# Attention's weights stay unscaled and are turned by a product with a diagonal matrix of reciprocal sums

## The reference

```python
# branch a (window_attention)
e = jnp.exp(s - m)
pr = e / (jnp.sum(e, axis=-1, keepdims=True) + jnp.exp(sk - m))
o = jnp.einsum('bnkgqs,bnskd->bnqkgd', pr.astype(v.dtype), v)
# branch b (dsa_attention)
pr = jax.nn.softmax(s, axis=-1)
o = jnp.einsum('bqkgs,bqskd->bqkgd', pr.astype(vg.dtype), vg)
```

## Time and profile before

| | |
|---|---|
| median of three runs | 1047.68 us |
| span of the profiled execution | 1044.9 us |
| PE busy | 930.3 us, 89% |
| PEld busy | 599.2 us, 57% |
| DVE busy | 394.1 us, 38% |
| ACT busy | 260.4 us, 25% |
| POOL busy | 123.1 us, 12% |
| attention | 162.4 to 257.2 us |

### The profile page before, as it was taken

The page is one execution under the profiler, slowest core; times in us unless marked ns, Lnnn a source line. Parts: engine busy times, 40 slices in busy tenths (PEclk is TensorE's granted clock), DMA queues, the critical chain, the costliest instruction groups (busy, mean ns, idle before and its releaser), DMA issues.

```text
span 1044.9 us, 14060 instructions
## 1 busy us (share of the span) xinstructions
PE 930.3 (89%) x5627; PEld 599.2 (57%) x5630; DVE 394.1 (38%) x1071; ACT 260.4 (25%) x529; POOL 123.1 (12%) x133
## 2 busy tenths in 40 slices
PE   7989998998999999998999977887987887887996
PEld 7869995456999998994333322332322222224885
DVE  4179998878242436453111101101101101101885
ACT  6254326675232323222000000000000000001541
POOL 2404730002030000001111111011010011000000
PEclk9999999999999999997999999999999999999998
DMA  8850602001925225356999999999999999996501
GB/s 262 115 153 2 201 2 61 1 1 30 299 62 158 65 61 241 127 206 249 430 425 425 426 429 427 424 429 424 427 426 427 425 427 428 425 428 250 211 26 60
DMA packets 60131, 263.71 MB, mean 252 GB/s; under 512 B 11054, under 2 KB 36030, under 8 KB 46224
## 3 DMA queue, kind: packets, MB, share of 16 engines
q1 hardware_dynamic: 54160, 250.99, 62.5%
q0 software_dynamic: 5296, 9.79, 2.6%
q10 hardware_dynamic: 624, 2.23, 0.6%
HBM read 253.99 MB, written 16.85 MB: 259 GB/s over the span
## 4 chain that ended last, share of the span: by engine, by line
PE 52%; DMA 30%; DVE 13%; ACT 2%; issue 2%; SPq 0%; DVEq 0%; ACTq 0%
DMA arena<-in_w_up 29%; PE ps L1083 13%; PE ps L1250 11%; PE ps L1115 4%; PE ps L1381 4%; DVE nrm L1901 4%; DVE hT L1905 3%; PE ps L871 3%; PE ps L1275 3%; PE ps L1365 2%; PE ps L1000 1%; PE ps L1049 1%; PE ps L1124 1%; PE ps L1028 1%; DVE xf L1905 1%
## 5 line engine op out<-in xcount | busy, mean ns | idle before, releaser
L1250 PE MATMUL ps<-arena,hT 128*64 128x512 f32 x992 | 243.7, 645 | 41.2 <-DMA arena<-in_w_up 41.0
L1250 PEld LDWEIGHTS ps<-arena,hT 128*64 128x64 f32 x992 | 74.5, 141 | 207.6 <-issue 157.5
L2185 DVE TENSOR_TENSOR xf<-xf,ps 128x256 f32<-128x256 f32 x32 | 13.5, 421 | 404.4 <-ACT xf L1666 379.0
L1083 PE MATMUL ps<-arena_merge,arena_merge 128*128 128x256 f32 x624 | 99.7, 287 | 0.0
L1275 PE MATMUL ps<-arena,xf 128*64 128x512 f32 x336 | 76.7, 598 | 12.8 <-DVE xf L2188 12.8
L1083 PEld LDWEIGHTS ps<-arena_merge,arena_merge 128*128 128x128 f32 x624 | 87.4, 188 | 0.0
L826 POOL DMA_INDIRECT expert_rows<-xf,arena x32 | 31.9, 998 | 427.0 <-ACT xf L1670 399.6
L1083 PE MATMUL ps<-xf_merge,arena_merge 128*128 128x256 f32 x480 | 82.0, 288 | 0.0
L1666 ACT ACTIVATE xf<-ps 128x256 f32<-128x256 f32 x30 | 11.5, 384 | 259.0 <-PE ps L1250 259.0
L1083 PEld LDWEIGHTS ps<-xf_merge,arena_merge 128*128 128x128 f32 x480 | 69.3, 188 | 0.0
L1670 ACT ACTIVATE xf<-ps 128x512 f32<-128x512 f32 x30 | 17.9, 597 | 159.8 <-PE ps L1275 159.8
(11 more groups left out here) (300 smaller groups left out, 1317.6 us busy)
## 6 DMA issues: line engine op xcount, KB each, us to landing
arena<-in_w_gate SPq DMA_DIRECT2D x30, 2048.0 KB, 30.0
arena<-in_w_up SPq DMA_DIRECT2D x30, 2048.0 KB, 37.5
arena<-in_w_down SPq DMA_DIRECT2D x11, 2048.0 KB, 37.3
hT<-in_w_down SPq DMA_DIRECT2D x11, 2048.0 KB, 36.5
arena<-in_w_down SPq DMA_DIRECT2D x20, 1024.0 KB, 31.5
arena<-in_w_in SPq DMA_DIRECT2D x10, 1024.0 KB, 6.4
arena<-in_w_in SPq DMA_DIRECT2D x3, 2048.0 KB, 9.9
arena<-in_w_gate SPq DMA_DIRECT2D x8, 512.0 KB, 10.2
```

The costliest lines, as they stand in the source:

```text
L1083: mm = pe.matmul(w[:, 2 * lo_t:lo_t + hi_t], rounded(st[:, c, cols]), rounded(mv[:, c, lo_t:hi_t]), start=c == 0 and k == 0, stop=c == pla ...
L1250: mm = pe.matmul(ps[g * BLK:(g + 1) * BLK, 2 + s, :], xsT[:, c, col:col + BLK], expert_columns(k, slice(0, 2), c, g), start=c == 0, stop=c ...
```

## The change

Step 5 falls away: `normalise`, `scale_weights`, `SCALERS` and the semaphores `p_ready` go. POOL gets a new step, `spread_inverse`: for each unit it multiplies the identity by the reciprocals, one for each row, and so writes a diagonal matrix of 128x128 to one of three buffers `inv_of`. It waits for the reciprocal, and from the fourth unit on until the unit three before is turned. In `turn` PE waits for the exponential and for this matrix, and instead of the transposition it makes an f32 product of the same tile with the matrix, which turns and scales at once. POOL's eight products `low` are spread: four go behind the matrices of units 53, 55, 57 and 59, four after the last. The buffers `inv_of` take 1.5 KB of each partition that nothing else uses in this stage. The whole diff:

```diff
@@ -181,14 +181,6 @@
     return COPIES[:u + 1].count(by)
 
 
-SCALERS = ['act' if _br == 'b' and ((_b == 3 and _j % 4 == 3) or (_b == 2 and _j % 2 == 1)) else 'dve' for _br, _b, _j in UNITS]
-
-
-def scaled(u):
-
-    return SCALERS[:u + 1].count(SCALERS[u])
-
-
 def unit_keys(br, b):
 
     if b == 's':
@@ -327,6 +319,7 @@
     pT_sb = [hb[:, 2048 * k:2048 * (k + 1)].rearrange("p (h b s n) -> p h b s n", h=KV, b=4, s=2) for k in range(2)]
     pT_s = [hb[:, 2048 * k:2048 * k + KV * 5 * P].rearrange("p (h b n) -> p h b n", h=KV, b=5) for k in range(2)]
     pr = [at(131.25 + 2.125 * k, [PAST + NS]) for k in range(3)] + [hb[:, 4 * D:4 * D + PAST + NS]]
+    inv_of = [at(137.625 + 0.5 * k, [P]) for k in range(3)]
     tab = at(131.25, [DIST])
     onehot = at(136.5, [DIST])
     relb = at(138, [16])
@@ -498,7 +491,7 @@
     kv_stored = sem("kv_stored")
     s_full, max_ready, exp_done = sem("s_full"), sem("max_ready"), sem("exp_done")
     inv_step = sem("inv_step")
-    p_ready = {by: sem("p_ready_" + by) for by in ('dve', 'act')}
+    inv_spread = sem("inv_spread")
     pt_full, pv_done, ot_out = (sem(n) for n in ["pt_full", "pv_done", "ot_out"])
     pt_out = {by: sem("pt_out_" + by) for by in ('dve', 'act')}
     chunk_in = [sem("chunk_in0"), sem("chunk_in1")]
@@ -793,10 +786,25 @@
                     link(pool.memset(dst[lo:lo + HD, plane(h), :], 0.0))
         pool.sem_inc(q_clean, 1)
 
-        for k in range(8):
+        def spread_inverse(u):
+            br, b, j = UNITS[u]
+            pool.wait_ge(inv_step, u + 1)
+            if u >= 3:
+                pool.wait_ge(pt_full, u - 2)
+            pool.tensor_scalar(inv_of[u % 3], ident[:, :], stat[:, 3, GROUP_OF[u], j:j + 1], None, ALU.mult)\
+                .then_inc(inv_spread, 1)
+
+        def output_low(k):
             pool.wait_ge(o_high, k + 1)
             low(oT[k // 4][:, k % 4, :], oT_hi[k // 4][:, k % 4, :]).then_inc(o_split, 1)
 
+        for u in range(len(UNITS)):
+            spread_inverse(u)
+            k, odd = divmod(u - UNITS_A, 2)
+            if odd == 1 and KD < k <= KD + 4:
+                output_low(k - KD - 1)
+        for k in range(4, 8):
+            output_low(k)
 
         def count(out, pattern, base, by_row=0):
             return pool.iota(out, pattern, base=base, channel_multiplier=by_row, allow_small_or_imprecise_dtypes=True)
@@ -1015,7 +1023,8 @@
         def turn(u):
             br, b, j = UNITS[u]
             n = unit_keys(br, b)
-            pe.wait_ge(p_ready[SCALERS[u]], scaled(u))
+            pe.wait_ge(exp_done, u + 1)
+            pe.wait_ge(inv_spread, u + 1)
             big = n > 512
             if u >= 1 and (big or unit_keys(*UNITS[u - 1][:2]) > 512):
                 wait_copied(u - 1)
@@ -1025,7 +1034,8 @@
             off = 0 if big else 512 * (u % 2)
             for k in range((n + P - 1) // P):
                 m = min(P, n - k * P)
-                mm = pe.transpose(w[0:m, off + k * P:off + (k + 1) * P], pr[u % 4][:, k * P:k * P + m], ident[:, :])
+                mm = pe.matmul(w[0:m, off + k * P:off + (k + 1) * P], pr[u % 4][:, k * P:k * P + m], inv_of[u % 3],
+                               start=True, stop=True)
             mm.then_inc(pt_full, 1)
 
         def weigh(u):
@@ -1520,12 +1530,6 @@
                 .then_inc(pt_out['act'], 1)
 
 
-        def scale_weights(u):
-            br, b, j = UNITS[u]
-            v = pr[u % 4][:, 0:unit_keys(br, b)]
-            act.wait_ge(inv_step, u + 1)
-            act.activation(v, v, ACT.Copy, scale=stat[:, 3, GROUP_OF[u], j:j + 1]).then_inc(p_ready['act'], 1)
-
         act.wait_ge(consts_in, 16 * CONSTS)
         for u, (br, b, j) in enumerate(UNITS):
             g, keys = GROUP_OF[u], unit_keys(br, b)
@@ -1533,8 +1537,6 @@
             v = pr[u % 4][:, 0:keys + (br == 'a')]
             act.activation(v, v, ACT.Exp, bias=stat[:, 0, g, j:j + 1], scale=-1.0,
                            accum_out=stat[:, 1, g, j:j + 1]).then_inc(exp_done, 1)
-            if u >= 1 and SCALERS[u - 1] == 'act':
-                scale_weights(u - 1)
             if u >= LAG and COPIES[u - LAG] == 'act':
                 copy_turned(u - LAG)
 
@@ -1977,12 +1979,6 @@
             dve.wait_ge(exp_done, u + 1)
             dve.reciprocal(inv, tot).then_inc(inv_step, 1)
 
-        def normalise(u):
-            br, b, j = UNITS[u]
-            v = pr[u % 4][:, 0:unit_keys(br, b)]
-            dve.wait_ge(inv_step, u + 1)
-            dve.tensor_scalar(v, v, stat[:, 3, GROUP_OF[u], j:j + 1], None, ALU.mult).then_inc(p_ready['dve'], 1)
-
         def copy_outputs(g):
             br, b, _ = UNITS[GROUP_UNITS[g][0]]
             o = oT[br == 'b']
@@ -2001,8 +1997,6 @@
                 row_max(u + 1)
             if 1 <= u <= len(UNITS):
                 invert(u - 1)
-                if SCALERS[u - 1] == 'dve':
-                    normalise(u - 1)
             if 2 <= u < len(UNITS) + 2 and COPIES[u - 2] == 'dve':
                 copy_turned(u - 2)
 
```

## The result

The changed kernel takes 1064.86 us (median of four), the kernel before 1047.95 on the same chip. One execution of the changed kernel was disturbed and took 3244.58 us; the other three took 1063.69, 1064.60 and 1065.11, and the ratio on record, 1.0172 with a 95% interval of 1.0147 to 1.0197, leaves it out. The forecast was 1056.7, within 1047 to 1064. The direction was right, and the size was half of what came: +16.9 us by the medians and +18.4 by the spans of the two profiled executions, where +9.0 were forecast.

What follows compares the result with a forecast made beforehand. The attention stage's chain of PE, ACT and DVE was taken as the bound, with no transfer in it. Stretch terms +0.8, +0.5, +4.6, +2.1 and +1.0 gave +9.0 us, so 1056.7 us, within 1047 to 1064.

Steps and rivals of the forecast that it cites:

- So POOL is hidden, by 0.1: Wait between attention units: with a 0.38 us diagonal, two units take 1.62 us against PE's own work of 1.71.
- the column rule: POOL's two-operand product at 2.1 ns a column, giving 0.49 us for a diagonal of 128 columns; 0.38 was taken.
- the loop: Shortest chain from one unit's turning to that of the unit two later: 1.33 us before, 1.62 after.
- B: Attention stage, rest of branch a, 256 keys each: bound by DVE and the handing over; forecast +0.5 us.
- A: Attention stage, first eight units of branch a: PE at half clock, so a tile pays double; forecast +0.8 us.
- C: Attention stage, 512- and 384-key units of branch b: bound by PE; +6.1 of work less 1.5 idle, forecast +4.6 us.
- D: Attention stage, the sample's two and the 256-key units: +3.1 for tiles, +1.1 POOL's products, -2.1 collision; forecast +2.1 us.
- E: Attention stage, 128-key units: +1.5 for tiles, half into idle time, last units pay POOL's diagonal; forecast +1.0 us.
- the -2.1 of the collision: DVE's scalings prolonged beside POOL's products: removing them was to give the stage back 2.1 us.
- the 0.64 of half clock: PE's work for a short unit, 0.43 + 0.21 us, used in pricing the rival with GpSimd as the bound.
- GpSimd as the bound: Rival: at 0.9 us a diagonal the loop takes 1.07 a unit, nothing hidden; +16.6 us, 1064.3; chance 0.12.
- The faster rival: DVE's relief outweighs PE's added work, mainly in B: -5.3 us, 1042.4; chance 0.08.

Runs made afterwards that it cites:

- e9: Changed kernel, but GpSimd writes only 32 of each diagonal's 128 columns, the rest being zero from before attention: 1059.58 us, ratio 1.0129.
- e4: Changed kernel with the identity as moving operand, without diagonals or the wait for them, division left out: 1054.30 us, ratio 1.0077.
- e1: Kernel before, but tiles are turned by an f32 product with the identity; scaling stays on DVE and ACT: 1058.46 us, ratio 1.0113.
- e10: Changed kernel with six buffers for the diagonals instead of three: 1063.26 us, ratio 1.0161.
- e7: Changed kernel, but all eight products of low parts stand on GpSimd behind the last diagonal: 1059.15 us, ratio 1.0125.
- e8: Kernel before, but GpSimd's eight products of low parts start only after attention has copied its last output: 1048.07 us, ratio 1.0011.
- e3: Changed kernel with tiles transposed again, without diagonals, the wait for them or the division: 1039.16 us, ratio 0.9931.
- e2: Changed kernel, but PE transposes with the identity, still waiting for GpSimd's now unused diagonals; division left out: 1050.92 us, ratio 1.0040.
- e6: Changed kernel, but GpSimd makes each diagonal twice, the first into a spare buffer: 1079.28 us, ratio 1.0324.
- e5: Changed kernel, but DVE makes each diagonal right behind its reciprocal, instead of GpSimd: 1056.86 us, ratio 1.0103.

## Why the prediction came out wrong

**The step that failed is "So POOL is hidden, by 0.1".** It had two faults. The first is the size: a diagonal is 0.607 us, not 0.38, twice the 0.287 of the selection that I leaned on and 0.12 over the 0.49 of the column rule. With it the prediction's own sum for the loop is 0.39 + 0.21 + 0.34 + 0.16 + 0.07 + 0.607 + 0.07 = 1.85 for two units, 0.14 over PE's 1.71. The second is the comparison: PE's own work for two units is no floor below which a longer way is free. With a diagonal of 0.37, at which the loop would again be hidden, B is still 33.5 us (e9), 1.5 above the 32.0 without any wait (e4). Taking the wait for the diagonal away altogether (e4) shortens after's stage by 9.5 us: A 3.2, B 2.0, C 0.2, D 1.4, E 2.7. The forecast had added 1.4 for it, 1.1 in D and 0.3 in E. A's 3.2 is mostly clock (PE's idle time there falls by 1.0, its busy time by 2.1, at 1.00 for 0.58). In B to E the wait was worth 6.3, and this is 4.9 more than the 1.4; the forecast's miss there is 6.1 (+14.3 measured, +8.2 forecast). So the wait taken for hidden is most of the miss. The size of a diagonal is the smaller fault: with it right, in e9, the stage is still 4.3 over the forecast.

Without its 1.4 the forecast was +7.6, and e4 measured +6.7. That nearness is partly luck: e4 has -1.2 in A, at a clock of 1.00, where +0.8 was forecast, and +2.4 in D, where 1.0 was.

By stretch, forecast against measured, with the part of the product (e1 less before) and of the diagonal (after less e1):

| | forecast | measured | product | diagonal | what was off |
|---|---|---|---|---|---|
| A | +0.8 | +1.9 | +0.4 | +1.5 | units of 0.64, little to hide a 0.607 behind; of the 1.5 some 0.5 goes with the lower clock or the buffers (e10) |
| B | +0.5 | +2.5 | +2.4 | +0.1 | a wait for a scaling stays, whoever makes it |
| C | +4.6 | +4.5 | +4.3 | +0.2 | nothing |
| D | +2.1 | +3.8 | +2.9 | +0.9 | the -2.1 of the collision didn't come |
| E | +1.0 | +3.4 | +1.3 | +2.2 | short units, and low parts in POOL's queue |
| rest | 0 | +2.0 | -0.1 | +2.1 | the granted clock, at the next stage's start and again later |

**Right.** A tile costs twice a transposed one, not four times: had the Trainium skill's four times as fast for the transpose mode in FP32 held here (TensorE: Matmul & The Clock Gate, section "Terms"), C would have grown by 57 x 0.165 - 1.5 = 7.9. C was bound by PE before, and paid: PE idle 0.36 of 34.24. B lies 2.5 above before, though, where "within 1.5" was to show the forecast. POOL's low parts cost 0.9 in D (e7), forecast 1.1. And the long scalings of DVE were the collision with POOL: without POOL beside them their mean is 0.353 (e8). The Trainium skill (SBUF — State Buffer, section "SBUF: two separate sides") has the two engines share a port pair as an exclusive lock, and the trace agrees: 0.441 with POOL beside them, 0.353 without.

**Wrong in its place.** The collision's 2.1 us were DVE's busy time, and I booked them as the stage's: e8 gave back 0.5. For B I wrote that 9.8 us for eight units follow from PE's work and the copies; e4, which waits for no diagonal, has 32.03 / 26 x 8 = 9.86. The wait made it 10.5. And the 0.64 of half clock that the prediction gives to A and E belongs to A alone: E was granted 1.00. What divides B's 2.4 in e1 between DVE, ACT and the hand-overs was not measured.

**The rivals.** GpSimd as the bound was priced at 1064.3 and given 0.12, and the time fell beside it. By stretch it was nearer than my forecast: +3.5, +2, +4.6, +3 and +3.5 against +1.9, +2.5, +4.5, +3.8 and +3.4. Yet it isn't simply the right one. It took 0.9 for a diagonal of 0.607, and the chain holds GpSimd only once in A and in E; the product alone is 11.4 of the 16.2. Too high a price for A makes up for too low ones in B and D, and that is luck. The faster rival had the relief right (6.4 us, e3), and failed on what took the scaling's place. Its point of decision, a reserve in B over 0.3 us a unit, wasn't reached: the product took 2.4 of B in e1.

**Behind the stage.** The first 32 matmuls of the next stage took 4.24 us before and 5.57 after. The 2 us ahead of them and the 4 us from them on, after:

```profile
271.57:273.57 2.00, 0.76 (x6) 0.23 (x5) 0.75 (x2) 0.28 (x1) 0.00 (x0) 0.88 0.00 0
273.57:275.57 2.00, 2.00 (x9) 2.00 (x10) 2.00 (x1) 0.00 (x0) 0.00 (x0) 0.50 0.26 49
275.57:277.57 2.00, 2.00 (x14) 2.00 (x14) 1.28 (x2) 0.00 (x0) 0.00 (x0) 0.77 1.06 333
```

The same places in e7:

```profile
269.33:271.33 2.00, 0.76 (x5) 0.23 (x5) 0.75 (x2) 0.28 (x1) 2.00 (x2) 1.00 0.00 0
271.33:273.33 2.00, 2.00 (x16) 2.00 (x17) 2.00 (x1) 0.00 (x0) 2.00 (x2) 1.00 0.33 45
```

After starts the next stage at 0.50, the 1.2 GHz level, with 9 matmul records in 2 us where e7 has 16. That is 1.3 us. Another 1.5 are lost at a second drop, 150 us later: from the first matmul of L1125 to that of L1134 15.3 us go by (418.70 to 433.98), from L1115 to L1124 in before 13.8 (401.02 to 414.82). Two of these stretches after, and the same place before:

```profile
423.00:425.00 2.00, 1.95 (x11) 1.75 (x10) 2.00 (x2) 0.14 (x1) 0.00 (x0) 0.57 1.02 434
425.00:427.00 2.00, 2.00 (x12) 2.00 (x12) 0.46 (x1) 0.00 (x0) 0.00 (x0) 0.58 1.00 426
```
```profile
407.00:409.00 2.00, 2.00 (x19) 2.00 (x19) 0.79 (x1) 0.00 (x0) 0.00 (x0) 1.00 1.00 426
```

Some 0.8 comes back further on, which makes the 2.0. The second drop is not the change's own: it is also in e3, which has neither product nor diagonals, and whose rest is 787.8. The first is in after, e2, e6 and e10, with 5.5 to 6.3 us for the 32 matmuls, and e2 and e6 still have a rest of 788.1 and 787.8. What PE did before it: in E it was idle 3.4 us of 13.88 in after (0.92 at the longest in one piece), and as much in e10, 4.4 in e2 and 5.9 in e6, and 1.5 to 2.5 in the nine kernels that kept 1.00. The busy time in the last 2 us ahead is the same 0.76 in after and e7, though, so what tips the clock stays open.

## What to carry to other kernels

Price an operation on another engine from a row of the same form (here a tensor by a column of scalars), or else carry the dear end of the bounds through the sum, since a time near the length of a unit decides between hidden and not. Work moved to an idle engine is hidden only if the way of a unit from one step to the next has slack; that engine's busy share, 12% for POOL here, says nothing of it. Before a product takes over a transposition, look whether PE bounds the stretch: in C its last 1.7 us of idle time went first, and the rest of the 6.1 us of work was paid. And look at the granted clock before a difference between two traces is given to an edit.

## What the runs showed of the hardware

- GpSimd takes 0.607 us for a 128x128 f32 tensor by a column of scalars and 0.371 for 128x32 (e9): by these two sizes, an estimate of (607 - 371) / 96 = 2.46 ns a column and about 0.29 us fixed. DVE takes 0.300 for the same 128x128 (e5).
- An f32 product of a 128x128 tile takes PE twice as long as its transposition: four tiles 0.89 us (after), two transposed ones 0.22.
- On this shape GpSimd is over twice as slow in that form as in its selection, 0.287; a shape alone doesn't give a price.
- A DVE scaling of 128x256 took up to 1.39 us beside a GpSimd product of 1.34 and 0.353 on average without; DVE's row maximum took the same 0.44 to 0.46 with GpSimd at work beside it (after) and without (e4).
- The granted clock of PE can be 0.50 at the start of a stage whose own code is unchanged: 32 matmuls took 5.57 us for 4.24. In stretch A the same 30 records took 4.33, 6.06 or 6.44 us at 1.00, 0.72 and 0.58.
